# A norm spread over sixteen slices, gate units ahead of the last key transposes, and convolution taps two units later

## What is computed

```python
def swiglu(h, w1, w3, w2):
    return (jax.nn.silu(h @ w1) * (h @ w3)) @ w2

def block(x, ...):
    h = rmsnorm(x, norm_ffn1) * (1.0 + m(1)) + m(0)
    x = x + 0.5 * m(2) * swiglu(h, w1_ffn1, w3_ffn1, w2_ffn1)
    h = rmsnorm(x, norm_mix) * (1.0 + m(4)) + m(3)
    mix, s_f, s_b = mixer(h, ...)
    x = x + m(5) * mix
    h = rmsnorm(x, norm_ffn2) * (1.0 + m(7)) + m(6)
    x = x + 0.5 * m(8) * swiglu(h, w1_ffn2, w3_ffn2, w2_ffn2)

# mixer: q, k, v, gate g, low-rank decay lr, and cb, cc, ch = slices of h @ w_in
#   o_gla  = rms(forward + backward gated linear attention) * silu(g)
#   u      = cc * ch
#   o_conv = cb * (w[0]*u[t-1] + w[1]*u[t] + w[2]*u[t+1])
#   mix    = concat(o_gla, o_conv) @ w_out
```

## Time and profile before

| | |
|---|---|
| median of 3 runs | 1367.88 us (1333.22 to 1456.43) |
| the profiled execution | 1334.19 us, of which the slowest core's span is 1332.7 us |
| spans of the eight cores | 1324.1 to 1332.7 us |
| PE busy | 1260.2 us, 95% of the span |
| DVE, ACT, POOL busy | 39%, 29%, 13% |
| chain that ended last | PE 87%, DMA 5%, DVE 3%, ACT 2% |

### The profile page before, as it was taken

The page is one execution under the profiler, slowest core; times in us unless marked ns, Lnnn a source line. Parts: engine busy times, 40 slices in busy tenths (PEclk is TensorE's granted clock), DMA queues, the critical chain, the costliest instruction groups (busy, mean ns, idle before and its releaser), DMA issues.

```text
span 1332.7 us, 18779 instructions; the slowest of 8 cores (1324.1 to 1332.7 us)
## 1 busy us (share of the span) xinstructions
PE 1260.2 (95%) x6592; PEld 570.7 (43%) x6592; DVE 519.2 (39%) x794; ACT 380.0 (29%) x625; POOL 179.9 (13%) x300
## 2 busy tenths in 40 slices
PE   2699999999998999899999989999999999999996
PEld 1244444444444444344444334444444444444442
DVE  2143243211331345576366645531243212432446
ACT  3354100111001244766435325621100111001343
POOL 3122001000010000123324222310001000000000
PEclk9899999999998999999999989999999999999998
DMA  9985456422569310002412213622313111020223
GB/s 176 224 185 79 80 85 94 76 32 32 91 92 151 97 64 1 1 1 53 76 24 51 86 37 90 110 49 42 59 27 62 34 32 32 0 48 1 61 63 130
DMA packets 33835, 90.93 MB, mean 68 GB/s; under 512 B 3888, under 2 KB 8400, under 8 KB 31568
## 3 DMA queue, kind: packets, MB, share of 16 engines
q0 software_dynamic: 21792, 62.01, 28.8%
q1 hardware_dynamic: 11952, 27.73, 6.4%
HBM read 137.04 MB, written 14.68 MB: 114 GB/s over the span
## 4 chain that ended last, share of the span: by engine, by line
PE 87%; DMA 5%; DVE 3%; issue 2%; ACT 2%; POOL 1%; DVEq 0%; ACTq 0%; SPq 0%; POOLq 0%
PE ps L235 87%; DMA sb_arena<-w_ada 3%; DVE sb_arena L263 2%; ACT sb_arena L248 2%; DMA sb_arena<-x 1%; DVE sb_arena L252 1%; PE ps L239 0%; POOL sb_arena L232 0%; POOL sb_arena L257 0%; ACT L248 0%; DVE sb_arena L730 0%; POOL sb_arena L252 0%; DVEq L141 0%; DVEq L1136 0%; ACTq L141 0%
## 5 line engine op out<-in xcount | busy, mean ns | idle before, releaser
L235 PE MATMUL ps<-sb_arena 128*128 128x512 bf16 (+4 forms) x5792 | 1204.1, 368 | 13.1 <-DVE sb_arena L252 5.4
L235 PEld LDWEIGHTS ps<-sb_arena 128*128 128x128 bf16 (+3 forms) x5792 | 534.9, 98 | 671.1 <-issue 62.2
L248 ACT ACTIVATE sb_arena<-ps 128x512 f32<-128x512 f32 (+3 forms) x272 | 161.1, 600 | 749.5 <-PE ps L235 743.6
L252 DVE TENSOR_TENSOR sb_arena<-sb_arena,ps 128x512 bf16<-128x512 f32 (+1 forms) x208 | 143.0, 688 | 505.3 <-PE ps L235 403.0
L263 DVE SCALAR_TENSOR_TENSOR sb_arena<-ps,sb_der,sb_arena 128x512 f32<-128x512 f32 x192 | 144.1, 751 | 160.7 <-PE ps L235 160.7
L248 ACT ACTIVATE sb_arena<-sb_arena 128x512 bf16<-128x512 f32 (+2 forms) x184 | 115.2, 678 | 39.3 <-DMA sb_arena<-x 17.7
L232 POOL DMA_DIRECT2D sb_arena<-w_ffn x88 | 47.1, 545 | 440.2 <-PE ps L235 410.1
L252 DVE TENSOR_TENSOR sb_arena<-sb_arena 128x512 f32<-128x512 f32 x96 | 64.5, 713 | 22.4 <-ACT sb_arena L248 22.4
L259 POOL TENSOR_SCALAR sb_arena<-sb_arena,sb_der,sb_modT 128x512 bf16<-128x512 f32 x44 | 39.8, 907 | 223.8 <-DVE sb_arena L252 192.7
L235 PE MATMUL ps<-sb_arena,sb_onesB 128*128 128x512 bf16 x144 | 42.4, 406 | 27.2 <-ACT sb_arena L248 25.5
L248 ACT ACTIVATE sb_arena<-sb_arena,sb_modT,sb_der 128x512 bf16<-128x512 f32 x48 | 39.0, 812 | 69.1 <-DVE sb_arena L252 55.5
(11 more groups left out here) (40 smaller groups left out, 157.7 us busy)
## 6 DMA issues: line engine op xcount, KB each, us to landing
sb_arena<-w_ffn POOLq DMA_DIRECT2D x44, 512.0 KB, 7.6
sb_arena<-w_ada POOLq DMA_DIRECT2D x36, 512.0 KB, 9.3
sb_arena<-w_ffn POOLq DMA_DIRECT2D x44, 256.0 KB, 9.9
sb_arena<-x SPq DMA_DIRECT2D x8, 1024.0 KB, 13.4
y<-sb_arena SPq DMA_DIRECT2D x32, 256.0 KB, 3.6
xspill<-sb_arena SPq DMA_DIRECT2D x4, 1024.0 KB, 3.9
sb_arena<-xspill SPq DMA_DIRECT2D x4, 1024.0 KB, 5.9
sb_arena<-w_cv POOLq DMA_DIRECT2D x12, 256.0 KB, 7.9
```

Of the source, the lines that this page charges most:

```text
L235: return P.add("pe", lambda e: e.matmul(out, lhsT, rhs, start=start, stop=stop), reads=flat(reads), writes=flat(writes))
L248: return P.add("act", lambda e: e.activation(out=out, in_=in_, func=func, **kw), reads=flat(reads), writes=flat(writes))
L252: return P.add(eng, lambda e: e.tensor_tensor(out=out, in0=in0, in1=in1, op=op), reads=flat(reads), writes=flat(writes))
```

## The change

A norm now has sixteen slices: the four squaring slices, two empty ones, all eight sums in one slice, one more empty one, and the eight applying slices. The last two key transposes no longer come right after phase A: two gate units stand ahead of the first, one gate unit between the two and one behind them. The rates of the fillers in the first chain (0.625 to 0.5) and in the first quarter of the first core (1.5 to 1.25) are lowered in return. The convolution's `taps` are called two units after their projection instead of one.

```diff
@@ norm_slices
             out = [(lambda k0=k0: squares(k0, 2)) for k0 in (0, 2, 4, 6)]
-            out += [lambda: stats(0, 4), lambda: stats(4, 4)]
+            out += [lambda: None, lambda: None, lambda: stats(0, 8)]
+            out += [lambda: None]
             out += [(lambda kc=kc: app(kc)) for kc in range(8)]
@@ after phase A
-        while late_kt:
-            ktok_unit(*late_kt.pop(0))
@@ conv_unit
             else:
-                after_units(1, taps)
+                after_units(2, taps)
@@ chain and core
-        chain(0, 0.625, 56)
+        filler(2.0)
+        for kt in late_kt:
+            ktok_unit(*kt)
+            filler(1.0)
+        chain(0, 0.5, 56)
         for i in range(8):
             load_cv(i)
-        dfr, ob = core(0, [1.5, 1.25, 1.25, 1.25])
+        dfr, ob = core(0, [1.25, 1.25, 1.25, 1.25])
@@ end of the fillers
             unit_done()
+        unit_done()
```

## The result

The changed kernel's median is 1358.32 us (1356.42 to 1378.91, 4 runs), beside 1352.05 for the kernel before (1333.22 to 1456.43, 4 runs). The ratio to the kernel before is **1.0175, 95% interval 1.0151 to 1.0198**: slower by about 23 us. The medians differ by less than that because disturbed runs, of which the kernel before had more, stand in a median and are left out of a ratio.

The account below looks back on a forecast made before the run. PE was busy for 95% of the span, so only its idle time and what follows counted. 10.5 + 5.1 - 1.2 - 3.4 + 9.3 + 4.9 - 5.0 + 2.0 = +22 on 1334.2 gave 1356 us, range 1336 to 1380.

Parts of the forecast that it names:

- Boundaries of the first feed-forward: Three block boundaries there: PE stalls 3.5 us each for a late tile 7, 10.5 idle plus 5.1 of clock.
- The serial chain of ACT, DVE and POOL: Norm of block 2, first feed-forward: queued steps from Exp at 88.4 to POOL's last apply at 101.7; PE wants tile 7 at 98.2.
- Phase A of block 1: Wait before block 3's sums goes (3.65 idle, 3.0 clock); last key unit waits for the Ln (2.5, plus 0.8): net -3.4.
- Block 3 of phase A: PE's first matmuls of block 3 meet late tiles from 4 on: 6.2 us idle plus 3.1 of clock, +9.3.
- Gate units: End of phase A: first gate unit waits 4.7 us for its weights against 2.85 before, plus 3.0 of clock: +4.9.
- Taps: Attention cores: five PE waits for DVE (5.4 us) and 1.7 of clock go, less 0.8; with lost cover, net -5.0.
- The lost cover at the end of the core of pair 1: No unit left between core 1's block 2 last products and its sums, which wait for two squares of ACT: 1.3 us.
- The clock rival: Every new gap leaves the lower clock as long as the 3.65 us wait did (3.0): +9, 1365 us; chance 0.30.
- My price of 1.7: Clock cost charged behind each feed-forward boundary gap, read from the 2.69 us wait before core 1: 1.7 us.
- The rival in which the clock holds: At all new gaps: the gaps come but the clock is not lowered, as after 1.19 and 1.66: 1344 us; chance 0.17.
- The rival in which the boundaries find their tiles in time: First feed-forward: the serial chain is shorter than added up, so 10.5, 5.1 and 9.3 go: 1331 us; chance 0.13.
- My other price, 3.0 us: Clock cost read from the aftermath of the 3.65 us wait in phase A, where eight matmuls take 3.62 us.

## Why the prediction was right or wrong

The time was forecast at 1356 with +22 us; it is 1358.32 and 1.0175, which is +23 on 1335. The waits came where the forecast put them, and most terms held. That the sum comes within 1 us of the result is in part luck, as the terms below show: errors of 1 to 2 us with either sign, and a clock that differs by several us from core to core.

**The step that failed** is the one from the sum to a verdict: "A measurement of this kernel tells about 2% (27 us) from no change, so this lies within 2%." I took the spread of the three runs shown, 1333 to 1456, for the uncertainty of a comparison. The interval of the ratio is 0.24% wide to either side, and even the part of 0.2% (3 us) above could be told from nothing. A sum of +22 us from eight terms, none of them near its size with the other sign, was a forecast of a slower kernel and should have been told as one; its number, 1356, also stood below the median shown of before, 1367.88, which was no base for it. With 0.67 on no change the chances said less than the working did.

**Boundaries of the first feed-forward: right.** Forecast 10.5 idle, 5.1 of clock, -1.2: 14.4. Measured 15.2 by leaving it out. In the rows the first block's -1.2 is not there: its waits are 5.1 us before and 4.8 here, with 1.9 and 2.7 of clock. The boundaries have 11.1 idle and 5.3 of clock. The serial chain of ACT, DVE and POOL is in the trace in the order and nearly with the times of the working: I had 13.3 us from the end of the Exp (88.4) to the end of POOL's last apply (101.7); it is 13.6 (94.63 to 108.23). At the second boundary the waits add up to 3.4 (forecast 3.5), at the first to 4.3. The table load at 96.42 takes 1.28 us; it begins 0.02 behind the end of the apply, and the Silu 0.01 behind the load. By the Trainium skill (ScalarE: Activation LUTs, What ACT_TABLE_LOAD costs) a switch of the set costs about 2.66 us, of which 1.38 are a drain beside the load; that would have made each boundary longer by up to an estimated 1.4. The trace does not agree.

**Phase A of block 1: mis-sized.** Forecast -3.4: a 3.65 us wait and 3.0 of clock against 2.5 and 0.8. The new wait is 3.66, with 1.7 of clock behind it, so the idle time is not shorter at all, and the 1.2 that the clock gives back is chance: on the mean of the eight cores the lower level cost 1.3 us there before and 1.2 here. I had the Ln 1.2 us too early. The norm of block 2 has two slices more, so the last four squares of block 3 come later, and stand on ACT right ahead of the four long Exps. The working had left them out. In ACT's order of time the first row holds both, four squares (2.2 us) and four Exps (4.1), without a break, and the Ln follows only then, while PE stood at the key unit from 590.2:

```profile
586.82 6.37 ACT L248 ACTIVATE sb_arena<-sb_arena 128x512 bf16<-128x512 f32 x8
...
593.10 0.58 ACT L248 ACTIVATE sb_arena<-ps 128x512 f32<-128x512 f32 x1
```

**Block 3 of phase A: right, a little large.** Forecast 6.2 idle in pieces of 1.3 to 2 and 3.1 of clock. The pieces are 5.3 together, with 3.6 of clock. The experiment that takes out this, the block above and the `down` units together gives 9.3, and the rows add up to 8.9: 8.9 lost here, 1.2 gained above, and two waits of 0.83 where 0.23 and 0.22 stood under the `down` units of the first pass (forecast 0.8 for both passes). Against my 5.9 and 0.8 the mis-sized wait is the largest difference, 2.2. At the end of the kernel, from the mark at the last `down` product, the tail takes 16.75 us against 16.28: +0.5, where I had 1.2.

**Gate units: right.** Forecast a wait of 4.7 and 3.0 of clock in place of 2.85; there are 5.51 and 2.6. PE went on 4.6 us behind the first load's issue (642.93), where I had 3.8 for its landing. Loading earlier gave back 7.3.

**Taps: right in sum, wrong in one step.** The waits for L252 fell from 5.4 to 1.8, and with the last taps in time the part is worth 0.54%, 7.2 us, against the 6.3 that I had of idle and clock. But I wrote that one unit later the edges "are there": in chain 1 DVE still waits about 1 us before each pair of taps, as this row of DVE in the whole change shows, where the earlier trace rows has 1.51.

```profile
753.57 1.61 DVE L263 SCALAR_TENSOR_TENSOR sb_arena<-sb_arena,sb_vec 128x512 f32<-128x512 f32 x2 [1.00 <-ACT sb_arena L248]
```

DVE waits for the middle tap on ACT now, 0.5 us less than for POOL's edges before. So one sign that I had named for a wrong prediction, DVE's idle time before the taps, half stays, and PE's waits went all the same; what slack the mask products still had is not measured. The lost cover at the end of the core of pair 1 cost 0.41 (forecast 1.3), and that same floor of the list is what keeps the last taps out of PE's way: I counted the price and did not see the use.

**The rivals.** The clock rival (1365) asked for the lower level behind every new gap, with 0.50 for more than 4 us behind a boundary. On the slowest core the lower level is there behind each of the new gaps that the forecast had, for 1.4 to 3.6 us of loss. At the second boundary its sign is met (2.6 us of loss are 5.1 us at the lower level), at the other two it is not. Over all eight cores the 24 boundary waits cost nothing three times, 1.3 to 1.7 us twelve times and 2.5 to 3.0 us nine times, 1.74 on average. My price of 1.7 was thus the right average of something that varies from 0 to 3; that it fitted the slowest core (5.3 against 5.1) was luck. The rival in which the clock holds is right at three waits in 24, and wrong as a whole. The rival in which the boundaries find their tiles in time is excluded: the waits for L259 stand on all eight cores.

My other price, 3.0 us behind the wait of 3.65 in the kernel before, was read on the slowest core alone. The same wait stands on all eight cores, and on four of them (hardware cores 0, 1, 2 and 4) it cost no clock. This is core 0, to be held against the earlier trace rows, where the four sums take 1.87 and the eight matmuls 3.62:

```profile
562.55 1.02 PE L235 MATMUL ps<-sb_arena,sb_onesB 128*128 128x512 bf16 x4 [3.65 <-ACT sb_arena L248]
...
563.41 1.89 PE L235 MATMUL ps<-sb_arena 128*128 128x512 bf16 x8
```

## What to carry to other kernels

An empty slot in a background list is not free: count how many slots there are before the first reader, and which engine's queue the last slice joins; here two more slices turned 0.8 us of slack into waits of 3.4 to 4.3 us at three boundaries. Work that is moved ahead as cover needs its own operands first: read the landing time of its load and the queue that issues it, then move the load with it. And when parts of a change have different signs, time them apart: here a version of 1.0175 held one gain (the taps, 0.54%) and another that appeared only once its load was moved (the gate units, 0.25%); with one slice placed otherwise they became 0.9889. And read on all cores what a gap costs in clock. In both kernels the slowest core is the one on which the lower level cost most (12.8 us before against a mean of 9.5, 21.8 in the change against 17.3), so its trace alone prices a gap too high.

## What the runs showed of the hardware that was not expected

The clock's price of a gap is not set by its length. The same wait of 2.51 us at the third boundary of the changed kernel left three cores (4, 5 and 6) at 1.00, cost four cores 1.3 to 1.6 us and one 2.6. The wait of 3.6 to 3.7 us ahead of the sums in phase A of the kernel before cost nothing on four cores, 1.7 us on one and 2.7 to 2.9 on three. The longest, 5.51 us for the gate weights, cost 2.6 on the slowest core. At waits that the change does not touch, two for `w_ada` ahead of tiny matmuls near 425 us before and near 442 here, the slowest cores paid 3.2 us before and 1.7 here. So a difference of 1 to 2 us between two single traces can be the clock alone; the ratios and the mean over the cores decide.

Filling the gaps settles it the other way: with twelve matmuls of 2.6 us whose result is thrown away in each boundary wait, the clock stayed at 1.00 on all eight cores behind waits of 2.1 us (first boundary) and 1.2 us (the other two), and the kernel was 0.36% faster.
